# A two-block transformer forward pass on one core: activation tables loaded earlier, the first two feed-forward products run in turn by parts, low halves made after all tiles are normed

## The chip, the cores and the metric

The kernel runs on one core of a Trainium2 chip. The metric is the device time of one execution in microseconds (us). The kernel before took 3234.5 us as the median of three runs (3233.2 to 3238.36).

## What is computed

The input is 512 tokens of width 1024. A first block with two layers puts 16 meta tokens ahead of them (528 positions), a second block with one layer follows. The parts that the change touches, cut from the reference:

```python
# first block, for each of 2 layers
u = rms_norm(h, ln_mix[l])                 # norm, then products of u @ w_in[l]
...                                        # four mixers, gates, merged
h = h + merged @ w_out[l]
u = rms_norm(h, ln_ffn[l])
h = h + (silu(u @ w_ffn_gate[l]) * (u @ w_ffn_up[l])) @ w_ffn_down[l]
# after both layers
x = rms_norm(h, ln_final)
# second block
h = modulate(rms_norm_2(x, g_pre_ff1), sh1, sc1)      # h * (1 + scale) + shift
x = x + 0.5 * ga1 * rms_norm_2(swiglu(h, w1_gate, w1_up, w1_down), g_post_ff1)
h = modulate(rms_norm_2(x, g_pre_mix), sh2, sc2)
...                                                    # attention and a state-space branch
mixed = concatenate([rms_norm_2(attn, g_attn_out), rms_norm_2(ssm, g_ssm_out)]) @ w_out
x = x + ga2 * rms_norm_2(mixed, g_post_mix)
h = modulate(rms_norm_2(x, g_pre_ff2), sh3, sc3)
x = x + 0.5 * ga3 * rms_norm_2(swiglu(h, w2_gate, w2_up, w2_down), g_post_ff2)
```

`rms_norm(x, g) = x * rsqrt(mean(x*x) + 1e-6) * g`. The feed-forward width is 2816.

## The kernel before, in words

**Tiles.** Activations stand transposed: 8 tiles of 128 features by 528 (or 512) tokens. A product of one weight slice (128 output features) is a job: 8 tiles of the depth, into one of three PSUM buffers (`NB = 3`, two banks each). 528 tokens go in two pieces of 264, 512 tokens in one.

**Split products.** Weights and inputs are each split into a high half (rounded to fp32r) and a low half (the rest, rounded too). A product is three matmuls for each tile of the depth: high by high, high weights by low inputs, low weights by high inputs. `split_lin` makes the three for a tile and goes on to the next tile; a product of 528 tokens is 48 matmuls of 264 columns, one of 512 tokens is 24 of 512. `staged_lin` goes over several products: all high by high first, then all low weights by high inputs, then all high weights by low inputs. It is used before only for the first three products of each layer.

**Weights.** SyncE streams them through a ring of four slots. ScalarE makes the high half of a load (`high_weights`, L1634), VectorE the low half in place (`low_weights`, L2079). There are two places for high halves. When product n has ended, ScalarE makes the high half of load n + 2 (`advance`), then VectorE its low half, and TensorE waits for that (`w_low`) before product n + 2.

**Norms.** ScalarE squares tiles (`square`, L1611), TensorE sums them over features by a matmul with a constant (`mean_square`, L1088), ScalarE takes the root (`root`, L1618), VectorE the reciprocal (`rinv`, L2028). Then VectorE multiplies each tile (`normed`, L2046), ScalarE makes its high half (`high_tile`, L1647 or L1649) and VectorE the low half (`low_tile`, L2062 to L2070).

**The four feed-forwards.** Each has 22 pairs of products (g for the gate, u for the other), in two halves of 11, each half followed by 8 down products. In the first block they are *scaled*: the products take the tiles of h times the gain, not normed, and the results are multiplied by 1/rms (L2107, L2110), so that the norm can run beside the first products. TensorE's order there is g of pair 0, the mean, u of pair 0, g of pair 1. VectorE's order is the reciprocal, the scaling of g, the low weights of g of pair 1; ScalarE's is the root, Silu of g (L1687), the high weights of g of pair 1. In the second block the tiles are normed first, and the low half of tile i - 1 is made behind the norm of tile i (`normed` with `split`).

**Order.** Every engine has its own program, written out by hand, and runs it in that order. Semaphores tie them. The compiler puts a load of an activation table before an activation whose function the loaded table does not hold; Square and Copy are in the tables used here, so none is loaded for them after another table.

Of the kernel before, what the change touches and what calls it, by code (L numbers as in the profile page):

```python
# [20 lines left out]
ACT = mybir.ActivationFunctionType  # L21
# [4 lines left out]
KT = D // P  # L26
# [221 lines left out]
def build(nc, ins, out_dram):  # L248
    with ExitStack() as ctx:
# [55 lines left out]
        def cell(n):  # L305
            at_small[0] += n
            return small[:, at_small[0] - n:at_small[0]]
# [9 lines left out]
        neghalf, epsc = cell(1), cell(1)  # L317
        onecol = cell(1)
        ostat = cell(20)
        dec = [cell(2) for _ in range(2)]  # L320


# [153 lines left out]
        S = {n: sem(n) for n in names}  # L476
# [547 lines left out]
        def _(pe):  # L1024
# [72 lines left out]
            def ffn(f, ada=None, ssm=False):  # L1097
                for half in range(2):
                    for i in range(FH * half, FH * half + FH):
                        g, u = f["pairs"][i]  # L1100
                        if ssm and i in TURN_AT:
                            turn_inputs(TURN_AT.index(i))
                        split_lin(g, f["x"]["is_low"] if i == 0 else ())
                        if i == 0 and f["scaled"]:
                            mean_square(f["norm"])
                        split_lin(u)
                        if ada is not None and 2 <= i < 20:
                            modulation(ada + i - 2)
                    for i, j in enumerate(f["down"][half]):
                        split_lin(j, [u.freed for _, u in f["pairs"][FH * half:FH * half + FH]] if i == 0 else ())  # L1110
# [380 lines left out]
            def second_block():  # L1491
                mean_square(b2["pre1"])
                ffn(b2["ffn1"], ssm=True)
                pe.wait_ge(S["bt_staged"], 2 * STEP)
                mean_square(b2["post1"])
                mean_square(b2["premix"])
                for i, j in enumerate(b2["u"]):
                    lin(j, [(S["u_shifted"], k + 1) for k in range(KT)] if i == 0 else ())
                wait(pe, b2["u"][-1].freed)
                state_space()  # L1500
                pe.wait_ge(S["proj_read"], 6)
                attention(*att2)
                wait(pe, (S["gelu_ready"], 4))
                pe.wait_ge(S["y_ready"], len(groups))
                for j in b2["glu"]:
                    lin(j)
                mean_square(b2["n_attn"])
                mean_square(b2["n_ssm"])
                for i, j in enumerate(b2["out"]):
                    split_lin(j, b2["x_out"]["is_low"] if i == 0 else ())  # L1510
                mean_square(b2["postmix"])
                mean_square(b2["pre2"])
                ffn(b2["ffn2"])
                mean_square(b2["post2"])
# [85 lines left out]
        def _(act):  # L1600
# [12 lines left out]
            def root(n, rinv_used=None):  # L1613
# [3 lines left out]
                    wait(act, rinv_used)  # L1617
                A(two(RINV, n["pieces"]), n["acc"], ACT.Sqrt, bias=epsc).then_inc(S["mean_read"], 1)  # L1618

            def squares(n, rinv_used=None):  # L1620
                for i in range(len(n["tiles"])):
                    square(n, i)
                root(n, rinv_used)
# [52 lines left out]
            def ffn(f, then=None, ssm=False):  # L1676
                if f["scaled"]:
                    root(f["norm"])
                else:
                    high_tiles(f["x"])  # L1680
                for half in range(2):
                    for i in range(FH * half, FH * half + FH):
                        g, u = f["pairs"][i]
                        if f["scaled"]:
                            gate = two(G[i % 2], f["pieces"])
                            wait(act, g.freed)
                            A(gate, gate, ACT.Silu).then_inc(S["silu_ready"], 1)  # L1687
                        else:
                            if i >= 2:
                                wait(act, f["pairs"][i - 2][1].freed)  # L1690
                            empty(g, two(G[i % 2], f["pieces"]), "act_ready", ACT.Silu)
                        advance(g.loads[0])
                        if ssm:
                            ssm_step(i)
                        advance(u.loads[0])
                    for i, j in enumerate(f["down"][half]):
                        advance(j.loads[0])
                        if half:
                            square(then, i)
# [200 lines left out]
            def first_block():  # L1900
                for ly in layers:
                    l = ly["l"]
                    if l == 0:
                        squares(ly["norm"])
                        for ld in ly["w"][0:3]:
                            high_weights(ld)
                    else:
                        high_weights(ly["w"][2])
                        root(ly["norm"])
                        act.wait_ge(S["h_stored"], 64)  # L1910
# [36 lines left out]
                    linear_attention(ly)  # L1947
                    high_weights(ly["out"][1].loads[0])
                    high_tiles(ly["xm"])
                    for i, j in enumerate(ly["out"]):  # L1950
                        advance(j.loads[0])
                        high_tile(ly["ffn"]["x"], i)
                        square(ly["norm_ffn"], i)
                    ffn(ly["ffn"], layers[1]["norm"] if l == 0 else norm_final)
                root(norm_final)
                act.wait_ge(S["params2_loaded"], 32)
                A(sc["dt"], pp("step"), ACT.Exp).then_inc(S["dt_ready"], 1)
                squares(b2["pre1"])
                ffn(b2["ffn1"], b2["post1"], ssm=True)
                root(b2["post1"])  # L1960
                squares(b2["premix"])
# [35 lines left out]
                    empty(j, two(G[i % 2], TOKENS), "gate_ready", ACT.Sigmoid, bias=pp("b_glu")[:, i:i + 1])  # L1997
                for j in b2["out"][0:2]:
                    high_weights(j.loads[0])
                squares(b2["n_attn"])  # L2000
                squares(b2["n_ssm"], b2["n_attn"]["done"][-1])
                high_tiles(b2["x_out"])
# [12 lines left out]
        def _(dve):  # L2015
# [26 lines left out]
            def normed(n, g, dst, shift=None, split=None):  # L2042

                a, z = rinv(n)
                for i, k in enumerate(n["tiles"]):
                    ins_ = V.scalar_tensor_tensor(out=dst[:, k, a:z], in0=n["src"][:, k, a:z], scalar=g[:, i:i + 1],  # L2046
                                                  in1=RINV[:, a:z], op0=ALU.mult, op1=ALU.mult)
                    if shift is not None:
                        link(ins_)
                        ins_ = V.tensor_scalar(dst[:, k, a:z], dst[:, k, a:z], shift[:, i:i + 1], None, ALU.add)  # L2050
                    ins_.then_inc(S[n["signal"]], 1)
                    if split is not None and i:
                        low_tile(split, i - 1)
                if split is not None:
                    low_tile(split, KT - 1)

            def low_tile(p, k):

# [794 lines left out]
```

## Time and profile before

| | |
|---|---|
| median of 3 runs | 3234.5 us (3233.2 to 3238.36) |
| the profiled execution, its own time | 3236.41 us |
| span of the profiled execution | 3234.3 us |
| TensorE (PE) busy | 3037.9 us, 94% |
| VectorE (DVE) busy | 1770.9 us, 55% |
| ScalarE (ACT) busy | 1016.3 us, 31% |
| GpSimd (POOL) busy | 220.5 us, 7% |
| mean granted TensorE clock | 0.967 |

A busy share is an average over stages. The time between the end of one instruction and the start of the next on the same engine is idle time; in square brackets behind a row stands that idle time and who ended it. The granted clock is 1.00 at TensorE's full speed and 0.50 at half of it.

### The profile page before, as it was taken

Reading aid. Unit: us, or ns where it says so; the run is one execution under the profiler, and the core shown is the slowest. Engines: PE = TensorE matmul, PEld = TensorE weight load, DVE = VectorE, ACT = ScalarE, POOL = GpSimd, SP = SyncE. Lnnn points to the kernel's source line nnn. Section 1 sums busy time; section 2 is a strip of 40 time slices with the busy share of each in tenths; the row PEclk is TensorE's granted clock in tenths of the full one; section 3 lists DMA queues with packets and bytes.
Section 4 is the critical chain, followed back from the end, with each engine's and each line's share of the span. In section 5 each row is a group of like instructions: output and inputs, shape, how many; then the busy total and the mean of one; then the engine's idle time right before and its main releaser. Section 6 shows DMA issues by size and latency. Waiting matters only on the chain.

```text
span 3234.3 us, 51830 instructions
## 1 busy us (share of the span) xinstructions
PE 3037.9 (94%) x21724; PEld 2592.7 (80%) x21724; DVE 1770.9 (55%) x3317; ACT 1016.3 (31%) x1745; POOL 220.5 (7%) x455
## 2 busy tenths in 40 slices
PE   7989999999999899999999999989999897789997
PEld 7867998999999897789897888858888554568886
DVE  4464577457556437457745756556447453553334
ACT  4655232241212246533224222233222214332221
POOL 0130222000000100222200000000000000000000
PEclk8989999999999999999999999989999998999999
DMA  5201121234433320112123544412334210113232
GB/s 177 99 15 47 50 67 59 66 131 162 163 118 127 127 78 28 47 42 67 58 73 131 170 162 137 144 53 92 113 115 171 102 37 19 63 65 106 89 100 70
DMA packets 74494, 302.47 MB, mean 94 GB/s; under 512 B 10728, under 2 KB 11112, under 8 KB 69272
## 3 DMA queue, kind: packets, MB, share of 16 engines
q1 hardware_dynamic: 57880, 230.04, 21.7%
q0 software_dynamic: 16384, 69.13, 6.0%
q8 instruction: 173, 2.83, 0.4%
q14 instruction: 57, 0.47, 0.0%
HBM read 288.51 MB, written 14.63 MB: 94 GB/s over the span
## 4 chain that ended last, share of the span: by engine, by line
PE 86%; DVE 8%; ACT 4%; issue 2%; DMA 0%; POOL 0%; ACTq 0%; DVEq 0%; SPq 0%
PE acc L1039 18%; PE acc L1040 18%; PE acc L1041 17%; PE acc L1301 5%; PE acc L1302 5%; PE acc L1303 5%; PE acc L1204 2%; ACT temps L1705 1%; PE acc L1073 1%; DVE work L2028 1%; PE acc L1058 1%; PE acc L1529 1%; PE acc L1178 1%; PE acc L1346 1%; PE acc L1151 1%
## 5 line engine op out<-in xcount | busy, mean ns | idle before, releaser
L1040 PE MATMUL acc<-normed_r,toep_r 128*128 128x512 f32 (+1 forms) x1824 | 643.7, 353 | 0.0
L1634 ACT ACTIVATE toep_r<-ring 128x1024 fp32r<-128x1024 f32 (+2 forms) x340 | 392.7, 1157 | 711.7 <-PE acc L1041 710.9
L2079 DVE TENSOR_TENSOR ring_r<-ring,toep_r 128x1024 fp32r<-128x1024 f32 (+2 forms) x340 | 458.1, 1349 | 263.3 <-ACT toep_r L1634 263.1
L1040 PEld LDWEIGHTS acc<-normed_r,toep_r 128*128 128x128 f32 x1824 | 345.3, 189 | 46.3 <-issue 0.2
L1039 PE MATMUL acc<-work_r,toep_r 128*128 128x512 f32 (+1 forms) x1024 | 354.7, 346 | 6.5 <-DVE temps_r L2070 6.3
L1041 PE MATMUL acc<-work_r,ring_r 128*128 128x512 f32 (+1 forms) x1024 | 353.6, 345 | 0.0
L1039 PE MATMUL acc<-mixed_r,toep_r 128*128 128x264 f32 (+1 forms) x1056 | 344.1, 326 | 5.1 <-DVE ring_r L2079 4.4
L1041 PE MATMUL acc<-mixed_r,ring_r 128*128 128x264 f32 (+1 forms) x1056 | 340.0, 322 | 0.0
L1039 PE MATMUL acc<-temps_r,toep_r 128*128 128x512 f32 x768 | 304.5, 396 | 24.7 <-DVE normed_r L2065 15.3
L1040 PE MATMUL acc<-work_r,toep_r 128*128 128x512 f32 (+1 forms) x880 | 307.3, 349 | 0.0
L1301 PE MATMUL acc<-residual_r,toep_r 128*128 128x264 f32 (+1 forms) x1024 | 303.0, 296 | 1.6 <-DVE mixed L2266 1.6
L1041 PE MATMUL acc<-temps_r,ring_r 128*128 128x512 f32 x768 | 302.0, 393 | 0.0
L1302 PE MATMUL acc<-normed_r,toep_r 128*128 128x264 f32 (+1 forms) x1024 | 293.8, 287 | 0.0
L1303 PE MATMUL acc<-residual_r,ring_r 128*128 128x264 f32 (+1 forms) x1024 | 292.6, 286 | 0.0
L1039 PEld LDWEIGHTS acc<-work_r,toep_r 128*128 128x128 f32 x1024 | 193.3, 189 | 31.7 <-issue 6.9
L1039 PEld LDWEIGHTS acc<-mixed_r,toep_r 128*128 128x128 f32 x1056 | 199.9, 189 | 20.2 <-issue 5.2
L1041 PEld LDWEIGHTS acc<-work_r,ring_r 128*128 128x128 f32 x1024 | 193.4, 189 | 24.5
L1041 PEld LDWEIGHTS acc<-mixed_r,ring_r 128*128 128x128 f32 x1056 | 200.2, 190 | 15.7
L1301 PEld LDWEIGHTS acc<-residual_r,toep_r 128*128 128x128 f32 x1024 | 197.8, 193 | 8.3 <-DVE mixed L2266 1.9
L1302 PEld LDWEIGHTS acc<-normed_r,toep_r 128*128 128x128 f32 x1024 | 197.7, 193 | 1.7
L1303 PEld LDWEIGHTS acc<-residual_r,ring_r 128*128 128x128 f32 x1024 | 197.7, 193 | 0.0
L1039 PEld LDWEIGHTS acc<-temps_r,toep_r 128*128 128x128 f32 x768 | 145.4, 189 | 64.8 <-issue 25.1
(398 smaller groups left out, 5363.0 us busy)
## 6 DMA issues: line engine op xcount, KB each, us to landing
ring<-in_w_pair SPq DMA_DIRECT2D x176, 512.0 KB, 3.5
ring<-in_w_down SPq DMA_DIRECT2D x64, 704.0 KB, 4.1
ring<-in_w_gb SPq DMA_DIRECT2D x64, 640.0 KB, 3.9
extra<-in_w_ada POOLq DMA_DIRECT2D x18, 1024.0 KB, 5.9
toep<-in_w_ada POOLq DMA_DIRECT2D x18, 1024.0 KB, 5.8
ring<-in_w_tm SPq DMA_DIRECT2D x24, 512.0 KB, 4.6
ring<-in_w_out SPq DMA_DIRECT2D x24, 512.0 KB, 3.5
ring<-in_w_fm SPq DMA_DIRECT2D x20, 512.0 KB, 4.0
```

The costliest lines, as they stand in the source:

```text
L1039: mm(out, wh, xh[:, a:z], start=i == 0, stop=False)
L1040: mm(out, wh, xl[:, a:z], start=False, stop=False)
L1041: last = mm(out, wl, xh[:, a:z], start=False, stop=end)
L1058: last = mm(PB[j.buf][:, s, 0:z - a], (wh, wl, wh)[stage], (xh, xh, xl)[stage][:, a:z], start=stage == 0 and i == 0, stop=stage == 2 and i ...
L1073: last = mm(PB[j.buf][0:j.rows, s, 0:z - a], w, x[:, a:z], start=i == 0, stop=i == len(j.terms) - 1)
L1151: last = mm(PS[0:rows, bank_of(c, g), col:col + k.shape[1]], x["q"], k, start=True, stop=True)
L1204: last = mm(PS[64 * j:64 * j + 64, 6, P * i:P * i + rows], v, x, start=b == 0, stop=b == k - 1, skip_group_check=True)
L1301: mm(out, wh, xh[:, a:z], start=m == 0, stop=False)
L1302: mm(out, wh, xl[:, a:z], start=False, stop=False)
L1303: last = mm(out, wl, xh[:, a:z], start=False, stop=m == len(xs) - 1)
L1634: A(high(ld), slot(ld), ACT.Copy).then_inc(S["w_high"], 1)
L2079: V.tensor_tensor(low(ld), slot(ld), high(ld), ALU.subtract).then_inc(S["w_low"], 1)
```

## The change

Four edits. `sqrt_table()` is a one-element square root on ScalarE, which makes the compiler put the table load in front of it; it stands at the start, ahead of the products of `out` in both layers, ahead of the last down products of each feed-forward, and ahead of the squares of the attention branch's norm in the second block. The exponential that makes `dt` moves behind the squares of `pre1`. The first pair of each feed-forward, and the first two products of `out` in the second block, go through `staged_lin`; with that the mean of a scaled feed-forward stands behind u of pair 0. The low halves in `normed` are made after all eight tiles.

```diff
+        rootc = cell(1)
...
                         if ssm and i in TURN_AT:
                             turn_inputs(TURN_AT.index(i))
-                        split_lin(g, f["x"]["is_low"] if i == 0 else ())
-                        if i == 0 and f["scaled"]:
-                            mean_square(f["norm"])
-                        split_lin(u)
+                        if i == 0:
+                            staged_lin([g, u], f["x"])
+                            if f["scaled"]:
+                                mean_square(f["norm"])
+                        else:
+                            split_lin(g)
+                            split_lin(u)
...
-                for i, j in enumerate(b2["out"]):
-                    split_lin(j, b2["x_out"]["is_low"] if i == 0 else ())
+                staged_lin(b2["out"][0:2], b2["x_out"])
+                for j in b2["out"][2:]:
+                    split_lin(j)
...
+            chain = [0]
+
+            def sqrt_table():
+
+                if chain[0]:
+                    act.wait_ge(S["scalar_chain"], chain[0])
+                A(rootc, onecol, ACT.Sqrt).then_inc(S["scalar_chain"], 1)
+                chain[0] += 1
...
                         advance(u.loads[0])
+                    if half:
+                        sqrt_table()
                     for i, j in enumerate(f["down"][half]):
...
                     if l == 0:
+                        sqrt_table()
                         squares(ly["norm"])
...
                     high_tiles(ly["xm"])
+                    sqrt_table()
                     for i, j in enumerate(ly["out"]):
...
                 root(norm_final)
+                squares(b2["pre1"])
                 act.wait_ge(S["params2_loaded"], 32)
                 A(sc["dt"], pp("step"), ACT.Exp).then_inc(S["dt_ready"], 1)
-                squares(b2["pre1"])
...
                 for j in b2["out"][0:2]:
                     high_weights(j.loads[0])
+                sqrt_table()
                 squares(b2["n_attn"])
...
                     ins_.then_inc(S[n["signal"]], 1)
-                    if split is not None and i:
-                        low_tile(split, i - 1)
                 if split is not None:
-                    low_tile(split, KT - 1)
+                    low_tiles(split)
```

TensorE around the first pair of the first layer's feed-forward, before: mixed_r and normed_r are the high and low halves of the inputs, toep_r and ring_r the high and low halves of the weights, L1088 is the mean.

```order
L1039 MATMUL acc<-mixed_r,toep_r 128x264 [waits x_low,w_low,h_done]
L1040 MATMUL acc<-normed_r,toep_r 128x264
L1041 MATMUL acc<-mixed_r,ring_r 128x264
...
L1088 MATMUL acc<-work,con 128x264 [waits sq_used,mean_read]
L1088 MATMUL acc<-work,con 128x264
L1088 MATMUL acc<-work,con 128x264 [waits sq_ready]
L1088 MATMUL acc<-work,con 128x264
L1039 MATMUL acc<-mixed_r,toep_r 128x264 [waits w_low,h_done]
```

And the same place now (L1089 is the mean, the row that waits for w_low and h_done behind it is g of pair 1).

```order
L1059 MATMUL acc<-mixed_r,toep_r 128x264 [waits x_high,w_high,h_done]
L1059 MATMUL acc<-mixed_r,toep_r 128x264 [waits x_high] x7
...
L1059 MATMUL acc<-mixed_r,ring_r 128x264 [waits w_low]
L1059 MATMUL acc<-mixed_r,ring_r 128x264 x15
L1059 MATMUL acc<-normed_r,toep_r 128x264 [waits x_low] x8
L1059 MATMUL acc<-normed_r,toep_r 128x264 x24
L1089 MATMUL acc<-work,con 128x264 [waits sq_used,mean_read]
L1089 MATMUL acc<-work,con 128x264
L1089 MATMUL acc<-work,con 128x264 [waits sq_ready]
L1089 MATMUL acc<-work,con 128x264
L1040 MATMUL acc<-mixed_r,toep_r 128x264 [waits w_low,h_done]
```

The mean stood between g and u of pair 0; now all 96 matmuls of both stand ahead of it, and g ends 16 matmuls before u does.

ScalarE between the gates of the second block and the root of the attention branch, before: the first two rows are high weights for `out`, the third the squares.

```order
L1634 ACTIVATE toep_r<-ring 128x1024 [waits lin_full2,w_ready2]
L1634 ACTIVATE toep_r<-ring 128x1024 [waits lin_full0,w_ready3]
L1611 ACTIVATE work<-mixed 128x512 [waits y_ready,sq_used] x4
L1618 ACT_TABLE_LOAD
L1618 ACTIVATE work<-acc,small 128x512 [waits sq_used]
```

The same place now.

```order
L1648 ACTIVATE toep_r<-ring 128x1024 [waits lin_full2,w_ready2]
L1648 ACTIVATE toep_r<-ring 128x1024 [waits lin_full0,w_ready3]
L1631 ACT_TABLE_LOAD
L1631 ACTIVATE small<-small 128x1 [waits scalar_chain]
L1616 ACTIVATE work<-mixed 128x512 [waits y_ready,sq_used] x4
L1623 ACTIVATE work<-acc,small 128x512 [waits sq_used]
```

The load moved from behind the four squares to ahead of them, with a small root behind it.

VectorE at the start of the second block's first feed-forward, before: L2028 is the reciprocal, L2046 the norm of a tile, L2065 its low half.

```order
L2028 RECIPROCAL work<-work 128x512 [waits mean_read,vector_chain]
L2046 SCALAR_TENSOR_TENSOR normed<-residual,small,work 128x512 [waits rinv_ready]
L2046 SCALAR_TENSOR_TENSOR normed<-residual,small,work 128x512
L2065 SCALAR_TENSOR_TENSOR normed_r<-normed,small,temps_r 128x512 [waits x_high]
L2046 SCALAR_TENSOR_TENSOR normed<-residual,small,work 128x512
L2065 SCALAR_TENSOR_TENSOR normed_r<-normed,small,temps_r 128x512 [waits x_high]
```

The same place now.

```order
L2047 RECIPROCAL work<-work 128x512 [waits mean_read,vector_chain]
L2065 SCALAR_TENSOR_TENSOR normed<-residual,small,work 128x512 [waits rinv_ready]
L2065 SCALAR_TENSOR_TENSOR normed<-residual,small,work 128x512 x7
L2082 SCALAR_TENSOR_TENSOR normed_r<-normed,small,temps_r 128x512 [waits x_high] x8
L2096 TENSOR_TENSOR ring_r<-ring,toep_r 128x1024 [waits w_high,act_ready]
```

Norms and low halves stood in turn; now eight norms stand ahead of eight low halves.

## Rows read from the trace of the kernel before

**Rows 1.** The page, part 4: shares of the chain that ended last, by engine.
```profile
PE 86%; DVE 8%; ACT 4%; issue 2%; DMA 0%; POOL 0%; ACTq 0%; DVEq 0%; SPq 0%
```

**Rows 2.** Timeline of ScalarE, program start: start us, length us, engine, line [idle before].
```profile
4.94 1.28 ACT L1611 ACT_TABLE_LOAD   x1 [4.94 <-DMA residual<-in_x]
15.69 1.28 ACT L1618 ACT_TABLE_LOAD   x1
```

**Rows 3.** Timeline, norm at the start of layer 1: the mean's last matmuls, the load.
```profile
1114.12 1.16 PE L1088 MATMUL acc<-work,con 128*128 128x264 f32 x4 [0.79 <-ACT work L1611]
1115.04 1.28 ACT L1618 ACT_TABLE_LOAD   x1
```

**Rows 4.** Table loads at roots (grouped by line), then the final norm's timeline.
```profile
L1618 ACT ACT_TABLE_LOAD x9 | 11.5, 1283 | 0.2
...
2146.51 1.13 PE L1088 MATMUL acc<-work,con 128*128 128x512 f32 x2 [0.89 <-ACT work L1611]
2147.77 0.69 ACT L1618 ACTIVATE work<-acc,small 128x512 f32<-128x512 f32 x1
```

**Rows 5.** Timeline, first pair of layer 0's feed-forward, by engine.
```profile
714.86 0.39 PE L1039 MATMUL acc<-mixed_r,toep_r 128*128 128x264 f32 x1 [0.64 <-DVE normed_r L2062]
718.27 1.94 PE L1088 MATMUL acc<-work,con 128*128 128x264 f32 x8
728.21 0.38 PE L1039 MATMUL acc<-mixed_r,toep_r 128*128 128x264 f32 x1 [2.16 <-DVE ring_r L2079]
...
712.77 0.72 ACT L1649 ACTIVATE mixed_r<-residual,par 128x528 fp32r<-128x528 f32 x1
720.25 0.70 ACT L1618 ACTIVATE work<-acc,small 128x528 f32<-128x528 f32 x1 [4.93 <-PE acc L1088]
...
720.99 3.46 DVE L2028 RECIPROCAL work<-work 128x528 f32<-128x528 f32 x1 [6.18 <-ACT work L1618]
726.84 1.23 DVE L2079 TENSOR_TENSOR ring_r<-ring,toep_r 128x1024 fp32r<-128x1024 f32 x1 [1.66 <-ACT toep_r L1634]
```

**Rows 6.** Timeline of TensorE, first pair of layer 1's feed-forward.
```profile
1770.16 1.88 PE L1088 MATMUL acc<-work,con 128*128 128x512 f32 x4
1779.89 0.77 PE L1039 MATMUL acc<-mixed_r,toep_r 128*128 128x512 f32 x1 [2.25 <-DVE ring_r L2079]
```

**Rows 7.** Timeline, attention branch's norm in the second block, and a small activation.
```profile
2727.50 0.20 ACT L1711 ACTIVATE small<-small 128x2 f32<-128x2 f32 x1
2751.30 1.99 ACT L1634 ACTIVATE toep_r<-ring 128x1024 fp32r<-128x1024 f32 x2
...
2753.95 3.80 PE L1088 MATMUL acc<-work,con 128*128 128x512 f32 x8 [3.34 <-ACT work L1611]
```

**Rows 8.** Timeline, start of the second block's first feed-forward.
```profile
2168.49 1.39 ACT L1647 ACTIVATE temps_r<-normed,small 128x512 fp32r<-128x512 f32 x2 [4.28 <-DVE normed L2046]
2170.15 0.77 PE L1039 MATMUL acc<-temps_r,toep_r 128*128 128x512 f32 x1 [6.75 <-DVE normed_r L2065]
...
2179.89 0.60 ACT L1627 ACTIVATE work<-acc 128x512 f32<-128x512 f32 x1 [0.54 <-PE acc L1041]
...
2181.54 1.23 DVE L2079 TENSOR_TENSOR ring_r<-ring,toep_r 128x1024 fp32r<-128x1024 f32 x1 [2.71 <-ACT toep_r L1634]
```

**Rows 9.** Stretches: length, PE busy (matmuls), granted clock, DMA share, GB/s.
```profile
2174.00:2176.00 2.00, 2.00 (x6) 0.58 0.00 0
2754.00:2756.00 2.00, 2.00 (x5) 1.00 0.00 0
2766.00:2768.00 2.00, 0.00 (x0) 0.55 0.00 0
2776.00:2778.00 2.00, 2.00 (x9) 0.89 0.00 0
```

**Rows 10.** Timeline, start of the second block's out products.
```profile
2769.72 2.62 ACT L1649 ACTIVATE temps_r<-normed 128x512 fp32r<-128x512 f32 x4 [2.13 <-DVE normed L2046]
...
2772.42 0.77 PE L1039 MATMUL acc<-temps_r,toep_r 128*128 128x512 f32 x1 [9.39 <-DVE normed_r L2068]
```

## The prediction

> **What bounds the kernel now.** I read the page's chain first: TensorE holds 86% of it, VectorE 8%, ScalarE 4% [rows 1]. So the time is TensorE's stream of matmuls, and the other two engines enter only where TensorE stands still. Next I took the timelines around every place that the diff names, and asked of each which wait ends last. The reader is to see three kinds of place: table loads that lie beside a matmul, table loads that lie alone, and a chain mean, root, reciprocal, weights that already ends after TensorE has run dry.
>
> **Table loads at roots.** There are nine before L1618, 1.28 us each [rows 4]. A load starts as soon as ScalarE's last instruction ends; only the root behind it waits for the mean. In the final norm the mean ends at 2146.51 + 1.13 = 2147.64 and the root starts at 2147.77: 0.13 late. In layer 0's feed-forward the root starts 0.04 after the mean's end at 718.27 + 1.94 = 720.21, so 0.04 stays, and taking the load away is worth 0.09, not 1.28 [rows 4, 5]. Five roots are of this kind (start, final norm, pre1, post1, post2): -0.45. Two, ahead of the scaled feed-forwards, had ended long before: ScalarE idled 4.93 us behind one [rows 5]: 0. In layer 1's first norm ScalarE made high weights first, so the load ends at 1116.32 while the mean ended at 1115.28: -1.0 [rows 3]. The ninth is the attention branch's, below. The new loads ahead of the down and out products lie in ScalarE's waits for TensorE: a product lasts 5.6 to 5.8 us [rows 5, 6] and ScalarE has some 2.4 us of work in it; if that cover were gone each would cost 1.28 + 0.20, but nothing here takes it. The moved exponential goes with its load behind the root of pre1, beside a reciprocal of 3.4 us: 0, and one load fewer.
>
> **The first load.** It stands behind the arrival of x, at 4.94 [rows 2]. Now it has no wait and runs while x is on its way: -1.28. The five roots above hold the second load of rows 2.
>
> The Trainium skill (ScalarE: Activation LUTs, What ACT_TABLE_LOAD costs) gives 1.28 us for the load and another 1.38 for a drain, 2.66 for each switch. The load's length agrees with rows 4; a drain doesn't show, since the root at 2147.77 follows the load at once. By the page's price the sum would be another one (rival D).
>
> **The load of the attention branch.** Before, it lay beside the last mean like the others. Now it stands between the high weights, which end at 2753.29, and the squares, on which TensorE already waits 3.34 us [rows 7]. Everything behind it moves: 1.28 + 0.20 for the small root (by the 128x2 activation in rows 7) - 0.09 for the place it leaves, with the hand-overs +1.5. TensorE's wait grows to 3.34 + 1.5 = 4.85 us. After 3.34 us the clock was still 1.00; a little later, after an idle that began at 2772.42 - 9.39 = 2763.03, it had fallen by 2766 to 2768 [rows 9, 10]. So the mean, 3.80 us at full clock, probably runs partly at half: between 0 and +3.8, I take +1.5. Root, reciprocal and four tiles are queued behind it.
>
> **The mean of the scaled feed-forwards.** This is the largest term. TensorE goes dry after u of pair 0: g of pair 1 waits 2.16 us for its low weights, and these wait for high weights, Silu, the scaling of g, the reciprocal (3.46 us), the root and the mean, since VectorE and ScalarE run in order [rows 5]. From the mean's end at 720.21 to g of pair 1 at 728.21 are 8.00 us, a fixed chain. The mean now stands behind u. u takes 728.21 - 2.16 - 720.21 = 5.84 us, so the mean ends 5.84 later and g of pair 1 starts 5.84 later. Besides, stage one of g needs the last high tile at 712.77 + 0.72 = 713.49, about 1.0 us after its turn, where the old order waited 0.64 [rows 5]: +0.36. Layer 0: +6.2. Layer 1: u takes 1779.89 - 2.25 - 1772.04 = 5.60, last tile 0.25: +5.85 [rows 6]. The half clock behind the restart is there before too (a wait of 2.16 us was enough), so I count it at 0 and keep -1 to +1 each. VectorE's later work (modulation, next weights) shifts with it and catches up. +12.05 together.
>
> **Starts of the second block's feed-forwards.** Before, TensorE starts at 2170.15, with the first low half; g ends at 2179.85, u 24 matmuls later. One matmul takes 5.60/24 = 0.233 us at full clock [rows 6], 0.46 at half. 2179.85 + 5.6 = 2185.45. Now the first high half is there at 2169.2 and the others every 0.70 us (1.39 for two); the eighth at 2174.05, its matmul done at 2174.5 [rows 8]. 40 are left. Until the eighth, TensorE is busy for 0.46 of each 0.70 us. The clock rose before near 2175.6, 5.4 us after the start, and for the out products near 2776.4, 4.0 us after [rows 9, 10]; I take 4 us from where TensorE is fully busy, 2178.5. Then 4.0/0.46 = 8.7 matmuls slow, 31.3 x 0.233 = 7.3: u ends at 2185.8, +0.35. Then comes what the turns cost: g ends only 8 matmuls, 1.86 us, before u, and behind g's end stand Silu, high and low weights, until 2181.54 + 1.23 = 2182.77, 2.92 us after g's end at 2179.85 [rows 8]. That lay beside u's 5.6 us; now 1.05 shows. +1.4 for this one, and as the second has the same rows of work in the same order, +1.2 there (bounds of each -0.5 and +2.5, by the moment at which the clock rises). +2.6.
>
> **Out products of the second block.** All high halves are there at 2769.72 + 2.62 = 2772.34, before TensorE's old start at 2772.42 [rows 10]. The first product's high part is then done but for one matmul; 40 are left at 2772.8 instead of 48 at 2772.42. With the rise at 2776.4 the old pair ends at 2785.6, the new one at 2783.9; the third product waits for its weights, 2.4 us behind the first product's end (the 2.92 above without Silu's 0.5) against 1.86 of cover: 2784.45. -1.1 (0 to -3.4, if the clock doesn't fall because TensorE starts near 2766).
>
> **Sum.** -1.28 - 0.45 - 1.0 + 1.5 + 1.5 + 12.05 + 2.6 - 1.1 = +13.8. Against the profiled execution's own 3236.41 (span 3234.3) that is 3250.2. The median of the runs shown is 1.9 lower, 3234.5: 3248.3. I say 3248.
>
> **Rivals.** A change of 0.2%, 6.5 us, is about what can be told from none.
>
> B, warm restarts: the clock holds in the attention branch's wait and at the out products. For it: 3.34 us were not enough to fall. Against it: rows 9 after 2763. 13.8 - 1.5 - 2.3 - 2.6 = +7.4: 3242.
>
> C, cold restarts: the mean of the attention branch wholly at half clock (+3.8 instead of 1.5), both starts +2.5, the scaled ones +1 each, nothing won at out. 13.8 + 2.3 + 2.4 + 2 + 1.1 = +21.6: 3256. For it: waits of 8 us instead of 2.2. Against it: the old restarts after long waits rose in 4.0 and 5.4 us.
>
> E, the scaled feed-forwards take the later mean without loss, as slack further on gives it back; the edit then does only what it does elsewhere. 13.8 - 12.05 = +1.7: 3236. Against it: the 2.16 and 2.25 us show that this chain ends last already.
>
> D, the other side: a switch of tables stops ScalarE for twice its row. Eight loads leave the chain (the first, and seven at roots), one comes back: 7 x 2.57 = 18.0 won, where I count 2.73, and 0.2 stays for the small root. -18.0 + 0.2 + 1.5 + 12.05 + 2.6 - 1.1 = -2.75: 3232. It decides from 2.2 us a switch on. Against it: nothing lies between load and root in rows 4. The rule of the Trainium skill (ScalarE: Activation LUTs, What ACT_TABLE_LOAD costs) is this one, and by its 2.66 the sum would be -3.4.
>
> **Chances.** Forecast 0.62, B 0.15, C 0.14, E 0.06, D 0.03. Slower than before by over 0.2%, from 3241: nearly all of the forecast, C, and two thirds of B: 0.85. Within: the rest of B, E, a little: 0.11. Faster: 0.04. The range leaves out E, D, and the end of C: 3240 to 3256; the forecast's own is 3243 to 3253.
>
> **What would show it.** Right: TensorE idle some 8 us between the mean and g of pair 1 in both scaled feed-forwards (was 2.2); the first square near 4.9; the root of the final norm 0.04 behind the mean; the attention branch's squares 1.5 us further from the high weights; in the second block's feed-forwards a wait of about 1 us ahead of g of pair 1. Wrong: if the 8 us aren't there, the forecast falls by 12; if roots come over 0.5 us sooner after the mean than now, table loads were worth more than I count.

## The result and the profile after

The changed kernel takes 3254.18 us as the median of 4 runs (3251.82 to 3256.26), beside 3234.56 for the kernel before on the same chip (4 runs, 3233.2 to 3238.36). The ratio is 1.0059, 95% interval [1.0041, 1.0076]: slower, by 19.6 us where I forecast 13.8. That is inside the range of 3240 to 3256, but 1.2 us above the forecast's own (3243 to 3253) and nearer to rival C's 3256 than to 3248. The profiled execution took 3256.26 us with a span of 3253.7 and a mean granted clock of 0.962, where it was 0.967.

TensorE still sets the time. The page's chain, its shares by engine, as in [rows 1]:

```profile
PE 87%; DVE 7%; ACT 4%; issue 2%; DMA 1%; POOL 0%; DVEq 0%; ACTq 0%; SPq 0%
```

To find where the 19 us are I laid the two traces side by side at the starts of VectorE's 13 reciprocals, one for each norm. Between two of them lies a stage; what differs is the table.

| from one norm's reciprocal to the next | before | after | difference | predicted |
|---|---|---|---|---|
| start of the program to the first | 17.79 | 16.38 | -1.41 | -1.37 |
| layer 0, to its feed-forward's | 703.20 | 709.46 | +6.26 | +6.2 |
| to layer 1's first norm | 396.07 | 395.41 | -0.66 | -1.0 |
| layer 1, to its feed-forward's | 655.74 | 666.10 | +10.36 | +5.85 |
| to the final norm | 375.69 | 376.04 | +0.35 | -0.09 |
| to pre1 | 15.83 | 16.07 | +0.24 | -0.09 |
| the second block's first feed-forward | 380.73 | 381.44 | +0.71 | +1.3 |
| premix to the attention branch | 196.31 | 199.11 | +2.80 | +3.0 |
| out products | 56.67 | 56.25 | -0.42 | -1.1 |
| the second feed-forward | 377.12 | 378.27 | +1.15 | +1.1 |

(The three left out differ by less than 0.02.) One line stands out: layer 1's stage grew by 4.5 more than its mean explains. The +6.26 of layer 0 has to be read with care, since this stage alone varies by 4 us from one profile of a kernel to the next (see `again`).

**The start.** Timeline of ScalarE, to be held against [rows 2]: the table load no longer stands behind x, and the first square starts at 5.05 instead of 6.24. The first reciprocal starts at 17.56 to 18.40 in the seven profiles of this document without the early load, and at 15.93 to 17.47 in the seven with it; the means are 17.85 and 16.52.

```profile
0.74 1.28 ACT L1631 ACT_TABLE_LOAD   x1 [0.74 <-PEq L2863]
5.05 1.18 ACT L1616 ACTIVATE work<-residual 128x528 f32<-128x528 f32 x2 [2.81 <-DMA residual<-in_x]
```

**The scaled feed-forward of layer 0.** TensorE's rows and then ScalarE's and VectorE's, which answer to [rows 5]. From the mean's end, 723.13 + 1.94 = 725.07, to g of pair 1 at 733.06 are 7.99 us, the chain of 8.00 of before, and now TensorE has nothing beside it.

```profile
712.15 3.33 PE L1059 MATMUL acc<-mixed_r,toep_r 128*128 128x264 f32 x25 [1.00 <-ACT mixed_r L1663]
723.13 1.94 PE L1089 MATMUL acc<-work,con 128*128 128x264 f32 x8
733.06 0.56 PE L1040 MATMUL acc<-mixed_r,toep_r 128*128 128x264 f32 x1 [7.99 <-DVE ring_r L2096]
...
725.11 0.70 ACT L1623 ACTIVATE work<-acc,small 128x528 f32<-128x528 f32 x1 [12.47 <-PE acc L1089]
...
725.84 3.45 DVE L2047 RECIPROCAL work<-work 128x528 f32<-128x528 f32 x1 [12.43 <-ACT work L1623]
731.69 1.22 DVE L2096 TENSOR_TENSOR ring_r<-ring,toep_r 128x1024 fp32r<-128x1024 f32 x1 [1.66 <-ACT toep_r L1648]
```

In layer 1 it is 7.85 us, where [rows 6] has 2.25:

```profile
1784.71 1.88 PE L1089 MATMUL acc<-work,con 128*128 128x512 f32 x4
1794.44 0.76 PE L1040 MATMUL acc<-mixed_r,toep_r 128*128 128x512 f32 x1 [7.85 <-DVE ring_r L2096]
```

**The attention branch's norm.** ScalarE's load and small root, then TensorE: the wait of [rows 7], 3.34 us, is 4.85, and the mean takes 5.37 instead of 3.80.

```profile
2768.97 1.28 ACT L1631 ACT_TABLE_LOAD   x1
2770.26 0.20 ACT L1631 ACTIVATE small<-small 128x1 f32<-128x1 f32 x1
...
2771.13 5.37 PE L1089 MATMUL acc<-work,con 128*128 128x512 f32 x8 [4.85 <-ACT work L1616]
```

**The second block's first feed-forward.** TensorE starts sooner after the norm, but in turns, and g of pair 1 waits 1.19 us for its low weights; this is the new wait of about 1 us, against [rows 8].

```profile
2184.50 7.90 PE L1059 MATMUL acc<-temps_r,toep_r 128*128 128x512 f32 x16 [5.87 <-ACT temps_r L1661]
2201.04 0.47 PE L1040 MATMUL acc<-temps_r,toep_r 128*128 128x512 f32 x1 [1.19 <-DVE ring_r L2096]
```

### The profile page after: what moved, and what is told of

Same layout as the page of the kernel before. It is cut to its first block, busy times and chain, and to the rows that moved or that the text cites. A ratio compares the mean times of both kernels' runs of the same rounds, so it can differ in the third digit from the quotient of the medians.

```text
span 3253.7 us, 51835 instructions
## 1 busy us (share of the span) xinstructions
PE 3051.8 (94%) x21724; PEld 2601.7 (80%) x21724; DVE 1770.4 (54%) x3317; ACT 1015.0 (31%) x1751; POOL 219.9 (7%) x455
## 4 chain that ended last, share of the span: by engine, by line
PE 87%; DVE 7%; ACT 4%; issue 2%; DMA 1%; POOL 0%; DVEq 0%; ACTq 0%; SPq 0%
PE acc L1040 17%; PE acc L1041 17%; PE acc L1042 17%; PE acc L1305 5%; PE acc L1306 5%; PE acc L1307 5%; PE acc L1059 3%; PE acc L1208 2%; PE acc L1074 1%; DVE work L2047 1%; ACT temps L1721 1%; PE acc L1182 1%; PE acc L1089 1%; PE acc L1534 1%; PE acc L1155 1%
## 5 line engine op out<-in xcount | busy, mean ns | idle before, releaser
L1041 PE MATMUL acc<-normed_r,toep_r 128*128 128x512 f32 (+1 forms) x1728 | 607.5, 352 | 0.0
L1041 PEld LDWEIGHTS acc<-normed_r,toep_r 128*128 128x128 f32 x1728 | 326.1, 189 | 43.8
L1040 PE MATMUL acc<-mixed_r,toep_r 128*128 128x264 f32 (+1 forms) x1008 | 328.3, 326 | 15.8 <-DVE ring_r L2096 15.8
L1042 PE MATMUL acc<-mixed_r,ring_r 128*128 128x264 f32 (+1 forms) x1008 | 324.9, 322 | 0.0
L1040 PE MATMUL acc<-temps_r,toep_r 128*128 128x512 f32 x720 | 282.2, 392 | 3.1 <-DVE ring_r L2096 3.1
L1042 PE MATMUL acc<-temps_r,ring_r 128*128 128x512 f32 x720 | 281.1, 390 | 0.0
L1040 PEld LDWEIGHTS acc<-work_r,toep_r 128*128 128x128 f32 x1024 | 193.4, 189 | 31.7 <-issue 6.9
L1040 PEld LDWEIGHTS acc<-mixed_r,toep_r 128*128 128x128 f32 x1008 | 191.2, 190 | 30.4 <-issue 17.0
L1042 PEld LDWEIGHTS acc<-mixed_r,ring_r 128*128 128x128 f32 x1008 | 191.3, 190 | 15.0
L1306 PEld LDWEIGHTS acc<-normed_r,toep_r 128*128 128x128 f32 x1024 | 198.7, 194 | 1.7
L1041 PEld LDWEIGHTS acc<-work_r,toep_r 128*128 128x128 f32 x880 | 165.2, 188 | 21.6
```

The costliest lines, as they stand in the source:

```text
L1040: mm(out, wh, xh[:, a:z], start=i == 0, stop=False)
L1041: mm(out, wh, xl[:, a:z], start=False, stop=False)
L1042: last = mm(out, wl, xh[:, a:z], start=False, stop=end)
L1306: mm(out, wh, xl[:, a:z], start=False, stop=False)
```

## The experiments

Times are compared on the same chip. There were three chips, with four kernels on each beside the kernel before: 3237.91 us for it (19 runs, 3232.34 to 3244.49) beside `again`, `mean_back`, `mean_late` and `tables`; 3234.65 (33 runs) beside `before_again`, `turns_second`, `mean_inside` and `tables_but_attn`; 3234.41 (23 runs) beside the other four. In each profile I read the same stages as above:

| kernel | layer 0 | to layer 1's norm | layer 1 | attention stage |
|---|---|---|---|---|
| before | 703.20 | 396.07 | 655.74 | 196.31 |
| before_again | 703.07 | 396.07 | 655.66 | 196.33 |
| turns_second | 699.08 | 396.11 | 655.63 | 195.90 |
| tables | 699.28 | 395.11 | 656.64 | 199.72 |
| tables_again | 699.11 | 395.12 | 659.87 | 199.83 |
| tables_but_attn | 700.52 | 395.07 | 659.80 | 199.04 |
| mean_inside | 696.76 | 395.15 | 659.30 | 196.37 |
| best | 700.29 | 394.12 | 660.28 | 199.06 |
| mean_back | 703.57 | 395.06 | 659.92 | 199.07 |
| mean_late | 709.34 | 396.58 | 664.79 | 199.11 |
| late_layer0 | 705.08 | 396.61 | 659.29 | 196.40 |
| late_layer1 | 699.20 | 396.12 | 661.25 | 199.09 |
| after | 709.46 | 395.41 | 666.10 | 199.11 |
| again | 705.23 | 395.45 | 666.09 | 199.12 |

### again

The changed kernel, unchanged.

> The changed kernel once more, to see what of its trace repeats. Theory P (clock by position): between layer 1's first norm and its feed-forward the changed kernel lost 4.2 us in code that the change does not touch, while the granted clock fell to half at other places than before; if that depends only on when each stage begins, the same loss is there again, within 1 us, and the time is 3252 to 3256. Rival N (chance of the one execution): the loss is between 0 and 8 us here, unlike 4.2.

3253.28 us, 4 runs, ratio 1.0041 [1.0026, 1.0056]. Layer 1's stage repeats to 0.01 us, and so do the later ones. Layer 0's stage is 4.2 us shorter. Laid side by side, the matmuls are 2.7 us further apart at 55 us than at 47: there one profile has half clock and the other full. Both stretches (length, PE busy and matmuls, granted clock, DMA share, GB/s), the changed kernel's first profile and then this one:

```profile
50.00:54.00 4.00, 4.00 (x21) 0.50 0.60 234
```

```profile
50.00:54.00 4.00, 4.00 (x35) 1.00 0.39 149
```

The same 4 us separate the profiles of kernels whose layer 0 is the old one (703.1 to 703.6 in three, 699.1 to 699.3 in four, 700.5 in `tables_but_attn`). A single profile of any of them carries that much chance in this stage.

### mean_back

```diff
-                        if i == 0:
+                        if i == 0 and f["scaled"]:
+                            split_lin(g, f["x"]["is_low"])
+                            mean_square(f["norm"])
+                            split_lin(u)
+                        elif i == 0:
                             staged_lin([g, u], f["x"])
-                            if f["scaled"]:
-                                mean_square(f["norm"])
                         else:
```

> The changed kernel with one part undone: in the two scaled feed-forwards g, mean, u as before (g and u by tiles, not in turn); all else as changed. Theory M (the place of the mean is the loss): the waits of TensorE ahead of g of pair 1 fall from 8.0 us to 2.2 in both, -12.1 us, to 3242; with the 4.2 us of layer 1 gone as well, if they come from the shift, 3238. Rival S (the turns themselves are slow): the time falls by under 4 us, since the turns in the second block stay.

3241.39 us (10 runs, 3237.2 to 3243.49), ratio 1.0004 [0.9994, 1.0013]: 11.9 below `again` on the same chip, where my term is 12.05; with runs 6 us apart the close agreement is in part luck. The stages say the same, 703.57 and 659.92 against 709.46 and 666.10: 5.9 and 6.2. The mean's place is the loss. But layer 1's stage is still 4.2 above the kernel before, so that part isn't the mean's.

### mean_late

```diff
                         split_lin(g, f["x"]["is_low"] if i == 0 else ())
-                        if i == 0 and f["scaled"]:
-                            mean_square(f["norm"])
                         split_lin(u)
+                        if i == 0 and f["scaled"]:
+                            mean_square(f["norm"])
```

> The kernel before with one part done: the mean of the two scaled feed-forwards behind u of pair 0, with g and u still by tiles. Theory M: +5.84 and +5.60 us, so 3246, and the waits ahead of g of pair 1 are 8.0 us. Rival S: the turns are needed for the loss, and the time stays within 3 us of before.

3252.53 us (4 runs), ratio 1.0042 [1.0027, 1.0057]: +14.6, where `again` has +15.4 on the same chip. This one move, in the old code, gives nearly the whole loss, so rival S (the turns are slow) falls. The stages show more than the 12 us of the two chains: +6.1 and +9.1, and +2.8 in the attention stage, where nothing was changed at all.

### tables and tables_again

All the early table loads and the moved exponential, products and lows as before.

> The kernel before with the table part alone: all sqrt_table() calls and the moved exponential. Theory T (a load counts only where nothing lies beside it): -1.3 at the start, -1.0 at layer 1's norm, -0.1 at four other roots, +1.5 to +3 in the attention branch of the second block: -1.2 to +0.5, so 3233 to 3235. Rival D (each switch stops ScalarE for twice its row): -15 or more, 3219.

3234.66 us (10 runs), ratio 0.9994 [0.9985, 1.0003]. So loads are not worth twice their row (rival D's 18 us don't come). Repeated on another chip:

> The kernel of the run named tables, unchanged: the early table loads alone. That run had layer 1's stage at 656.6; the same program with one load fewer, 1,400 us further on, had 659.8. If the clock's places belong to the program, this one has 656.6 again within 0.1 and 3234.7. If they are drawn anew in each run, it comes out at either 656.6 or 659.8, whatever the program.

3239.49 us (11 runs), ratio 1.0016 [1.0007, 1.0025]: the same program, and the intervals don't meet. The profiles show how that can be. In layer 1 TensorE waits 2.99 us for VectorE, until 1431.50 in the one and 1431.45 in the other, and the clock falls at different points: behind the wait in the first, inside it in the second. TensorE's row, then the stretches around it (granted clock ahead of the last two columns), first of `tables`:

```profile
1431.50 0.42 PE L1368 MATMUL acc<-work 64*16 64x16 f32 x20 [2.99 <-DVE work L2423]
```

```profile
1429.00:1431.00 2.00, 0.00 (x0) 1.00 0.00 0
1431.00:1433.00 2.00, 1.34 (x32) 0.89 0.00 0
1433.00:1435.00 2.00, 2.00 (x11) 0.50 0.00 0
1435.00:1437.00 2.00, 2.00 (x13) 0.76 0.00 0
1437.00:1439.00 2.00, 2.00 (x19) 1.00 0.01 4
```

Then of `tables_again`:

```profile
1431.45 0.45 PE L1368 MATMUL acc<-work 64*16 64x16 f32 x20 [2.99 <-DVE work L2423]
```

```profile
1429.00:1431.00 2.00, 0.00 (x0) 0.55 0.00 0
1431.00:1433.00 2.00, 1.55 (x28) 0.50 0.00 0
1433.00:1435.00 2.00, 1.84 (x13) 0.50 0.00 0
1435.00:1437.00 2.00, 2.00 (x8) 0.50 0.00 0
1437.00:1439.00 2.00, 2.00 (x11) 0.50 0.01 4
1439.00:1441.00 2.00, 2.00 (x17) 0.89 0.00 0
```

From these means the first has half clock from 1432.6 to 1436.0, the second from 1429.2 to 1439.4. Laid side by side, the second's matmuls lose 1.9 us here, and another 0.7, 0.4 and 0.2 us near 1600, 1640 and 1715 us, where the clock falls at other points too.

Layer 1's stage has two lengths by this, 3.2 to 3.6 us apart. The kernel before has the shorter one and the changed kernel the longer one (granted clock 0.58 in 1440 to 1442 us and 0.50 in the 8 us behind it).

What TensorE did before the wait sorts the two. I measured from the clock's last rise to the start of the wait. The stretches that hold the rise, of `tables` and then of `tables_again`:

```profile
1377.80:1378.00 0.20, 0.20 (x3) 0.66 0.00 0
```

```profile
1377.80:1378.00 0.20, 0.20 (x3) 0.55 0.00 0
```

The rises are at 1377.94 and 1377.98, the waits start at 1428.51 and 1428.46: 50.57 and 50.48 us. In all 14 profiles the five with the short form have 50.51 to 50.61 us, and the clock falls 4.0 to 4.1 us after the wait's start, behind it. The nine with the long form have 50.16 to 50.48 us, and it falls 0.7 to 1.0 us after the wait's start, inside it. The sorting was found afterwards, no run set this distance on purpose, and why the longer distance is the cheaper one is not shown.

The loads show something else too. The root of layer 1's first norm is 1.0 us sooner (395.11), but the stage behind it is 0.9 longer than the kernel before's (656.64), although both have the short form: together 1051.75 against 1051.81. TensorE restarts 5.91 us after the mean instead of 6.92, but at half clock, and full clock is back at the same distance. The stretches that hold the rise, `before` (mean's end at 1115.28) and then `tables` (1109.59):

```profile
1130.00:1132.00 2.00, 2.00 (x14) 0.70 0.00 0
```

```profile
1124.00:1126.00 2.00, 2.00 (x13) 0.66 0.00 0
```

A mean of 0.70 is 1.2 us at half and 0.8 at full, so the rise is at 1131.2, 15.9 us behind the mean; 0.66 puts it at 1125.4, 15.8 behind. The 1.0 us of work added is done at half clock: about half of it is lost (0.4 us by the starts of the same matmuls). The other half goes further on. Behind a wait of 1.75 us `tables` has half clock again, where the kernel before, with the same wait 6 us later by its own time, keeps full clock; 1.3 us are lost there and 0.9 of them won back in the next 30 us. TensorE's row and the stretch behind it, `tables` and then `before`:

```profile
1211.33 0.59 PE L1176 MATMUL acc<-con,temps 128*16 128x128 f32 x2 [1.75 <-DVE temps L2231]
```

```profile
1212.00:1214.00 2.00, 2.00 (x11) 0.50 0.00 0
```

```profile
1217.64 0.38 PE L1175 MATMUL acc<-con,temps 128*16 128x128 f32 x2 [1.74 <-DVE temps L2216]
```

```profile
1218.00:1220.00 2.00, 2.00 (x20) 1.00 0.00 0
```

The changed kernel does the same at both places (0.5 and 0.5 us).

### tables_but_attn

The kernel of `tables` without one of its loads; against `tables` the edit is:

```diff
-                sqrt_table()
                 squares(b2["n_attn"])
```

> The kernel before with all the early table loads except the one ahead of the attention branch's squares in the second block. By my rows: -1.28 (first load), -0.45 (five roots), -1.0 (layer 1's first norm) = -2.7, so 3231.8, and the stage up to that norm's reciprocal 3.0 us shorter than in the run with that load (199.72 us there, 196.3 expected here). Rival: the load costs nothing there and the 3.4 us of that stage are the clock's own play: 3234.5 and 199.7.

3239.04 us (11 runs), ratio 1.0014 [1.0005, 1.0023]. I expected 3231.8 and an attention stage of 196.3; it is 199.04. Both the theory and the rival miss. The wait is back to 3.34 us, but now the clock falls in it, and the mean takes 6.46 instead of 3.80.

`late_layer0` and then `late_layer1` show the two cases in kernels that have no load there either, TensorE's row of the mean and the stretch that holds the clock's last rise before it:

```profile
2759.96 3.80 PE L1088 MATMUL acc<-work,con 128*128 128x512 f32 x8 [3.34 <-ACT work L1614]
```

```profile
2744.90:2745.10 0.20, 0.20 (x2) 0.83 0.00 0
```

```profile
2756.52 6.46 PE L1088 MATMUL acc<-work,con 128*128 128x512 f32 x8 [3.34 <-ACT work L1614]
```

```profile
2741.60:2741.80 0.20, 0.20 (x1) 0.85 0.00 0
```

From the rise (2744.97 and 2741.66) to the start of the wait are 11.65 and 11.52 us. The same distance sorts all nine profiles without the load: 11.65 to 11.89 us in the five whose clock held, 11.52 to 11.55 in the four whose clock fell inside the wait.

### turns_second

The products by turns and the later low halves in the second block alone.

> The kernel before with only the products by turns in the second block's two feed-forwards and its out products, tiles normed first and low halves behind. By the comparison of stages: +0.7, +1.15 and -0.4, together +1.4 us: 3236. My prediction's own terms were +1.4, +1.2, -1.1 = +1.5. Rival: the starts lose only in company of the moved loads, 3234.5 and each stage within 0.2 us of before.

3233.99 us (11 runs), ratio 0.9999 [0.999, 1.0008]. By stages +0.62, -0.63 and +1.15: 1.14 together, 1.44 in the changed kernel; the time can't show it. The rival (no loss without the moved loads) falls by the stages. The attention stage is 0.4 us shorter, which I did not follow.

### before_again

> The kernel before, unchanged, profiled once more. Theory P (the granted clock follows the place of the work in a fixed program): layer 1's stage, between the reciprocals of its two norms, is again 655.7 us within 0.2, and later stages too; the first stage may differ by some 4 us as it did between two runs of the changed kernel. Rival N (chance): that stage comes out anywhere between 655.7 and 660.

3234.57 us (10 runs). Layer 1's stage 655.66, the attention stage 196.33, the later ones within 0.1. For this program theory P holds in two profiles of two; for `tables` it does not.

### late_layer0 and late_layer1

The edit of `mean_late` in one layer each.

> The kernel before with the mean behind u in layer 0's feed-forward alone. Theory P (a later place of the work changes at which of the untouched waits the clock falls): +6.2 there by the chain, and layer 1's stage between the reciprocals of its two norms goes from 655.7 to about 660 though nothing in it is changed, and the second block's stage ahead of the attention branch's reciprocal from 196.3 to 199.1: together +13, 3247.5. Rival L (each layer pays for its own later mean alone): +6.2, 3240.7, and the stages stay at 655.7 and 196.3.

3246.2 us (6 runs), ratio 1.0033 [1.0021, 1.0044], +11.8. Layer 1's stage is 659.29, the long form, though only layer 0 was touched, against rival L. It is one profile, but the time agrees: the fastest of the six runs is 10.5 us above the fastest of the kernel before, where the chain alone gives 6. The attention stage kept 196.40, which P had at 199.1.

> The kernel before with the mean behind u in layer 1's feed-forward alone. Up to that feed-forward it is the kernel before, so layer 1's stage must be 655.7 + 5.85 = 661.6. Theory P leaves open whether the attention branch's stage of the second block is 196.3 or 199.1: 3240.4 or 3243.2. Rival L: 3240.4 and 196.3.

3244.38 us (6 runs), ratio 1.0031 [1.0019, 1.0042], +10.0. Layer 1's stage is 661.25: 5.6 for the chain and the short form, as in every profile whose program is the old one up to there (4 of 4; of the ten others only `tables`). The attention stage is 199.09. The sum of the differences by stage, 5.6 + 0.5 + 0.4 + 2.8 + 0.5 (out) = 9.8, meets the 10.0.

### mean_inside and best

```diff
                         last = mm(out, wl, xh[:, a:z], start=False, stop=end)
+                    if s == 0 and norm is not None:
+                        mean_square(norm)
...
-                        split_lin(g, f["x"]["is_low"] if i == 0 else ())
-                        if i == 0 and f["scaled"]:
-                            mean_square(f["norm"])
+                        split_lin(g, f["x"]["is_low"] if i == 0 else (),
+                                  f["norm"] if i == 0 and f["scaled"] else None)
```

> The kernel before, with one edit: the mean of the two scaled feed-forwards runs inside g of pair 0, behind its first piece (24 matmuls), not behind g. Theory M (a fixed chain of 8.0 us from the mean's end to g of pair 1): the mean ends 3.1 us sooner in layer 0, so the chain ends before u does and g of pair 1 waits 0 instead of 2.16 us; in layer 1 0 instead of 2.25. The half clock that followed the waits (some 14 matmuls at 0.21 instead of 0.12 us, 1.8 us) goes with them: -4.0 us in each layer, 3226.5. Rival W, g of pair 1 is held by its weights or by a transfer anyway: the wait stays, 3234.5. Rival K, the clock falls somewhere else in its place: the waits are gone but only -4.4, 3230.

3236.54 us (11 runs), ratio 1.0005 [0.9997, 1.0014]. The expectation held an error: g of layer 1 has one piece, so behind its first piece is behind g, where the mean stood. Only layer 0 was changed. There the mean is done at 712.04 + 1.94 = 713.98, VectorE's low weights at 721.83, and g of pair 1 has no wait, at full clock:

```profile
712.04 1.94 PE L1090 MATMUL acc<-work,con 128*128 128x264 f32 x8
...
720.61 1.22 DVE L2080 TENSOR_TENSOR ring_r<-ring,toep_r 128x1024 fp32r<-128x1024 f32 x1 [1.66 <-ACT toep_r L1635]
```

```profile
724.00:726.00 2.00, 2.00 (x18) 1.00 0.68 244
```

Against before, ScalarE's instructions stand 3.3 us sooner ahead of this place (the chance of the first stage) and 7.2 sooner behind it: 3.9 us won, where I had 4.0. And layer 1's stage is 659.30, the long form, which takes 3.6 of it. The time shows nothing.

> The early table loads without the attention branch's, and the mean of the scaled feed-forwards inside g of pair 0. By the terms alone: -2.7 for the loads and 2 x -4.0 for the waits of 2.16 and 2.25 us and the half clock behind them: 3223.8. By what the two edits gave apart, where layer 1's untouched waits took back 4 to 6.6 us and the attention branch's mean 2.7: 3231. Rival: the clock gives back everything, 3234.5 or more.

`best` has the loads of `tables_but_attn` and this mean: 3236.01 us (11 runs), ratio 1.0006 [0.9997, 1.0015]. The wait is gone here too, and the two untouched places both have their longer form (660.28, 199.06). No kernel that I ran beats the kernel before. Two ideas are left that I did not run: the mean inside g of layer 1, and matmuls on constants in TensorE's waits, to see whether work of any kind holds the clock.

## Why the prediction came out as it did

- **Mean behind u, +12.05.** Right, in mechanism and size: 7.99 and 7.85 us idle, 5.9 and 6.2 by stages and 11.9 by time between `mean_back` and the changed kernel.
- **Table loads.** First load and roots right (-1.41 at the first reciprocal for -1.37, and -1.33 between the means of seven profiles each). D fell: by it `tables` would be some 16 us faster than before (its 18.0, less 1.7 for the attention branch), and it was 3.3 faster on one chip and 5.1 slower on another. The price of 2.66 us a switch in the Trainium skill (ScalarE: Activation LUTs, What ACT_TABLE_LOAD costs) is not seen here. At layer 1's norm -1.0 was mis-sized: the reciprocal is sooner, the layer is not. Half of it was lost at half clock behind the restart and half at a wait 85 us further on (1211 us in `tables`), behind which the clock fell once more. I priced the earlier restart as if every matmul behind it kept its clock.
- **The attention branch, +3.0.** The stage says +2.8, the idle is 4.85 us to the hundredth, and the mean's +1.5 came out as 1.57, yet that the load costs this much is only half right. With the load that stage was 199.07 to 199.83 in five profiles. Without it, it was 195.90 to 196.40 in five and 199.04 to 199.11 in four, by whether the clock fell in the 3.34 us. So the load costs some 3 us where the clock would have held, and 0.8 where it falls anyway (`tables_again` beside `best`, 199.83 and 199.06, both with 11.55 us from the last rise to the wait). I took "after 3.34 us the clock was still 1.00" for a property of the wait; it was one of two outcomes, and 0.1 us in the distance from the last rise sorts them.
- **Starts and out products.** +0.71 and +1.15 for +1.4 and +1.2, -0.42 for -1.1, the new wait 1.19 for 1.05: right in kind, all near what can't be told in time.
- **Missed.** 4.5 us of layer 1's stage. By the starts of the same matmuls in `before` and the changed kernel, 4.3 of it lie ahead of the feed-forward, in code that the change doesn't touch: 1.0 is the norm's returned gain, 1.9 are lost at the wait of 2.99 us, and 0.7, 0.4 and 0.25 near 1600, 1640 and 1720 us. No term of mine and no rival had it: B and C put the clock only where the change puts work, and the sum has nothing for work that merely moves in time. That a change in layer 0 alone brings it is shown by `late_layer0`. What decides it isn't the kernel alone (`tables` did both), not the wait's length (equal), and not the time in the program (1431.50 and 1431.45). What sorts all 14 profiles is how far the wait starts behind the clock's last rise: the two groups lie 0.03 us apart, and the two profiles of `tables` differ by 0.09. What sets that distance, and whether it is the cause or goes along with it, is not shown.
- **The range.** The time fell inside it by its width. The stages add up to 19.4 us; without the 4.5 that no term has they would be 14.9. With it the time looks like rival C, whose mechanism isn't there: C has the attention branch's mean at +3.8 for 1.57, and the starts at +2.5 each for 0.71 and 1.15.

## What to carry to other kernels

When a step at the head of a chain (mean, root, reciprocal, scaling, weights) is moved behind a product, and TensorE already waits at the chain's end, the whole product is added to the time: read that wait first. And read every wait of some 2 to 3 us in the kernel, not only those near the change: the three that were followed here (1.75, 2.99 and 3.34 us) have two prices each. A change of a few us may be won where it was made and lost 700 us later, so compare stage by stage, in more than one profile, before believing a gain or a loss under 0.3%: layer 0's 4.2, layer 1's 3.6 and the attention stage's 2.8 us add up to that.

## What was not expected of the hardware

- Equal waits with unequal outcomes: in a wait of 2.99 us the granted clock fell to half after 0.7 to 1.0 us, or only 1.0 us behind its end; after 3.34 us idle the mean took 3.80 or 6.46 us.
- The distance from the clock's last rise to the wait sorts these outcomes without an exception: above 50.5 us or below it in 14 profiles, 11.65 to 11.89 or 11.52 to 11.55 us in nine.
- Repeats are nearly exact where the clock takes the same way: layer 1's stage 666.10 and 666.09, the last feed-forward of the kernel before 377.12 and 377.10.
- Layer 0's stage varies by 4.2 us between two profiles of one kernel, 2.7 of it by the clock between 47 and 55 us.
- The same kernel against the same other kernel was 0.9994 [0.9985, 1.0003] on one chip and 1.0016 [1.0007, 1.0025] on another.
